# A two-block network on one core: in the second block the convolution's columns ahead of the keys, its norm beside the value and query projections, first scores ahead of the last query projection, one reciprocal for two heads

## The reference, cut to what matters

```python
h  = modulate(rmsnorm(x),   shift, scale)        # the block's tokens
hc = modulate(rmsnorm(ctx), shift_c, scale_c)    # 256 context tokens
z  = h @ w_in                                    # columns: q | k | v | gate u, gate v | conv a, conv gate
kc, vc = keys and values of hc                   # from the same columns k and v
att = softmax(q k^T / 8 + bias | q kc^T / 8) (v | vc)            # 8 heads of 64
sg  = gelu(u) * (w_s @ layernorm(gelu(v_s)) + b_s)               # spatial gating, 256 wide
cv  = silu(group_layernorm(dwconv31(a * sigmoid(gate)), 4 groups))   # 256 wide
x = x + mod * (concat(att, sg, cv) @ w_out)
x = rmsnorm(x + mod * conv_ffn(modulate(rmsnorm(x), ...)))
```

## Time and profile before

| | |
|---|---|
| median of three runs | 872.05 us |
| profiled execution | 870.56 us |
| its span on the core | 869.3 us |
| PE busy (share of the span) | 842.5 us (97%) |
| PE weight loads | 734.1 us (84%) |
| DVE busy | 600.8 us (69%) |
| ACT busy | 430.1 us (49%) |
| mean granted PE clock | 0.992 |
| second block's projections | 521 to 592 us of the span |
| attention | 592 to 634 us |
| output projection up to the feed-forward | 634 to 672 us |

### The profile page before, as it was taken

One profiled execution on the slowest core, in us unless ns is written; L12 is line 12 of the kernel. 1 busy time (PEld: TensorE's weight loads), 2 busy tenths in 40 slices (PEclk: granted clock), 3 DMA queues, 4 the chain that ended last, 5 costly groups with the idle time before them and its releaser, 6 DMA issues.

```text
span 869.3 us, 13540 instructions
## 1 busy us (share of the span) xinstructions
PE 842.5 (97%) x5555; PEld 734.1 (84%) x5555; DVE 600.8 (69%) x834; ACT 430.1 (49%) x662; POOL 52.7 (6%) x72
## 2 busy tenths in 40 slices
PE   9999999999999999999999999997898999999996
PEld 7988988869989999999988779984465999999995
DVE  7754547556698688688685765897766855665564
ACT  7555434446436646645636534634654644444432
POOL 8200004410000000000000000000000000000000
PEclk9999999999999999999999999999999999999999
DMA  8979865764543443345346776545446455555531
GB/s 286 322 228 269 237 213 213 274 220 150 157 131 107 135 146 118 126 146 178 113 146 211 261 260 241 197 146 178 161 170 218 134 175 180 191 194 188 176 121 49
DMA packets 102632, 160.10 MB, mean 184 GB/s; under 512 B 11317, under 2 KB 67993, under 8 KB 100266
## 3 DMA queue, kind: packets, MB, share of 16 engines
q1 hardware_dynamic: 102570, 159.24, 55.4%
HBM read 156.02 MB, written 3.21 MB: 183 GB/s over the span
## 4 chain that ended last, share of the span: by engine, by line
PE 81%; DVE 11%; ACT 3%; POOL 2%; issue 2%; DVEq 1%; POOLq 0%; ACTq 0%
PE acc L442 12%; PE acc L444 12%; PE acc L443 12%; PE acc L471 8%; PE acc L473 8%; PE acc L472 8%; PE misc L1167 4%; PE misc L2133 2%; PE misc L2135 2%; PE misc L2134 2%; DVE AT L1189 2%; DVE w_lo L415 2%; PE misc L854 2%; DVEq L1188 1%; PE misc L982 1%
## 5 line engine op out<-in xcount | busy, mean ns | idle before, releaser
L415 DVE TENSOR_TENSOR w_lo<-raw,w_hi 128x2048 fp32r<-128x2048 f32 x114 | 262.5, 2315 | 121.4 <-ACT w_hi L408 121.2
L408 ACT ACTIVATE w_hi<-raw 128x2048 fp32r<-128x2048 f32 x114 | 217.4, 1910 | 101.4 <-PE misc L2135 28.0
L442 PE MATMUL acc<-XH,w_hi 128*128 128x256 f32 x848 | 242.1, 286 | 1.1 <-DVE XL L597 1.1
L443 PE MATMUL acc<-XL,w_hi 128*128 128x256 f32 x848 | 240.3, 283 | 0.0
L444 PE MATMUL acc<-XH,w_lo 128*128 128x256 f32 x848 | 240.3, 283 | 0.0
L442 PEld LDWEIGHTS acc<-XH,w_hi 128*128 128x128 f32 x848 | 163.1, 192 | 3.8 <-issue 3.0
L443 PEld LDWEIGHTS acc<-XL,w_hi 128*128 128x128 f32 x848 | 163.1, 192 | 0.8
L444 PEld LDWEIGHTS acc<-XH,w_lo 128*128 128x128 f32 x848 | 163.0, 192 | 0.0
L471 PE MATMUL acc<-w_hi,XH 128*128 128x512 f32 (+1 forms) x224 | 87.4, 390 | 0.0
L473 PE MATMUL acc<-w_hi,XL 128*128 128x512 f32 (+1 forms) x224 | 85.7, 383 | 0.0
L472 PE MATMUL acc<-w_lo,XH 128*128 128x512 f32 (+1 forms) x224 | 85.5, 382 | 0.0
(11 more groups left out here) (284 smaller groups left out, 1282.9 us busy)
## 6 DMA issues: line engine op xcount, KB each, us to landing
raw<-in_hgrn_w_in_dram SPq DMA_DIRECT2D x32, 1024.0 KB, 5.5
ada_raw<-in_ada_w_dram SPq DMA_DIRECT2D x24, 1024.0 KB, 7.2
raw<-in_ffn_w_up_dram SPq DMA_DIRECT2D x22, 1024.0 KB, 5.0
raw<-in_pool_w_in_dram SPq DMA_DIRECT2D x15, 1024.0 KB, 6.0
raw<-in_ffn_w_down_dram SPq DMA_DIRECT2D x11, 1024.0 KB, 5.0
raw<-in_w_in_dram SPq DMA_DIRECT2D x10, 1024.0 KB, 5.4
raw<-in_pool_w_out_dram SPq DMA_DIRECT2D x8, 1024.0 KB, 5.1
raw<-in_hgrn_w_out_dram SPq DMA_DIRECT2D x8, 1024.0 KB, 5.1
```

The costliest lines, as they stand in the source:

```text
L408: self.hi_done.up(act.activation(self.w_hi[v % RING][:, 0:w], self.raw[j][:, 0:w], ACT.Copy), v)
L415: self.lo_done.up(dve.tensor_tensor(self.w_lo[j][:, 0:w], self.raw[j][:, 0:w], self.w_hi[v % RING][:, 0:w].bitcast(F32), ALU.subtract), v)
L442: pe.matmul(o, wh[:, k, c:c + P], xh[:, k, :], start=k == 0, stop=False)
L443: pe.matmul(o, wh[:, k, c:c + P], xl[:, k, :], start=False, stop=False)
```

## The change

It touches the second block only, and no product is added or left out.

- **Units.** The keys' slab has four tiles (the context's) instead of eight. The convolution follows; a new slab `kx` without units of its own reads the keys' two units again for the block's tokens, behind the convolution. So the order of loads is the same, and the keys' units stay in use longer.
- **`out1`.** The splits of the convolution's two units move ahead of each half's copy of turned tokens on ACT and behind each half's low part on DVE. PE turns the two halves after the second and the third context key.
- **`in2`.** PE: context keys, convolution, keys, gates, values; the context's value tiles are cut so that the group sum of the taps comes after the first unit of both, and the sum of the squares between the second units. The norm of the convolution, its silu and split run on DVE and ACT beside the value and query projections; the sum of squares is written over `CP`. The gating's layernorm takes two instructions per half instead of three. The first scores come ahead of the last query tile.
- **`attention`.** No group sums. One reciprocal takes the sums of both heads of a step. The low halves of convolution and gating follow step 0. Of the output projection's units DVE splits one ahead of the loop, and the other three after steps 1, 4 and 6; ACT splits its last two after steps 2 and 4. Modulation product 15 moves from step 1 to step 2.
- **`out2`.** Gating and convolution are taken first in every tile, the last heads last.

```diff
-        self.u_k = slab(8, *by_column(w_in2, 512))
+        self.u_k = slab(4, *by_column(w_in2, 512))
         self.u_cv = slab(4, *by_column(w_in2, 2048))
+        self.u_kx = slab(4)
+        self.slab[self.u_kx] = self.slab[self.u_k]
...
         for half in range(2):
+            self.hi(self.first(u0 + half, 3) + RING)
             for c in range(2):
                 self.act_high("in2", half, c, self.XH)
             self.act_context_key(2 + half)
-        self.hi(self.first(u0, 3) + RING)
-        self.hi(self.first(u0 + 1, 3) + RING)
...
             for c in range(2):
                 self.dve_low("in2", half, c, self.XH, self.XL)
-        self.lo(self.first(u0, 3) + RING)
-        self.lo(self.first(u0 + 1, 3) + RING)
+            self.lo(self.first(u0 + half, 3) + RING)
...
         for n in range(4):
             self.project(k, n, n * P, HC, KD)
-            if n == 3:
+            self.pe_ada(KD + n)
+            if n in (1, 2):
                 for c in range(2):
-                    self.pe_turn("in2", 0, c, self.XN2)
-            self.pe_ada(KD + n)
-        for c in range(2):
-            self.pe_turn("in2", 1, c, self.XN2)
+                    self.pe_turn("in2", n - 1, c, self.XN2)
         for n in range(4):
-            self.project(k, 4 + n, n * P, X, KD, self.both_ready("in2") if n == 0 else None)
+            self.project(cv, n, n * P, X, KD, self.both_ready("in2") if n == 0 else None)
         for n in range(4):
-            self.project(cv, n, n * P, X, KD)
+            self.project(kx, n, n * P, X, KD)
...
-        self.project_tokens(v, (2, 3), self.slab[v], 0, 512, HC)
+        self.project_tokens(v, (2, 3), self.slab[v][:1], 0, 512, HC, K=KD)
+        self.pe_group_mean()
+        self.project_tokens(v, (2,), self.slab[v][1:], 0, 512, HC, K=KD)
+        self.pe_group_square()
+        self.project_tokens(v, (3,), self.slab[v][1:], 0, 512, HC, K=KD)
...
         for n in range(4):
             self.project(q, n, n * P, X, KD)
+            if n == 2:
...
+                pe.wait_ge(self.V.h, self.V["gated2"])
+                self.pe_scores(0)
...
+        self.conv_taps(0, 8)
+        self.lo(self.first(k, 0) + RING)
+        self.conv_taps(8, 12)
+        self.lo(self.first(k, 1) + RING)
...
+        self.conv_taps(12, 16)
+        self.lo(self.first(cv, 0) + RING)
+        self.conv_taps(16, 18)
+        self.lo(self.first(cv, 1) + RING)
...
+        self.conv_taps(18, TAPS)
...
+        dve.wait_ge(self.A.h, self.A["cv_root"])
+        t = V.up(dve.reciprocal(self.CS, self.CS))
...
-    ADA_BESIDE = ((12, 13), (14, 15), (), (16,), (17,), (18,), (19,), ())
+    ADA_BESIDE = ((12, 13), (14,), (15,), (16,), (17,), (18,), (19,), ())
...
     def dve_normalize(self, s):
-        dve, V = self.nc.vector, self.V
+        dve, V, n = self.nc.vector, self.V, s % 2 * 2
+        dve.wait_ge(self.A.h, self.A["e", s, 1])
+        t = V.up(dve.reciprocal(self.soft[:, n:n + 2, 2:3], self.soft[:, n:n + 2, 1:2]))
+        dve.wait_ge(V.h, t)
         for e in range(2):
-            n = s % 2 * 2 + e
-            dve.wait_ge(self.A.h, self.A["e", s, e])
-            t = V.up(dve.reciprocal(self.soft[:, n, 2:3], self.soft[:, n, 1:2]))
-            dve.wait_ge(V.h, t)
...
+            if s == 0:
+                self.dve_mix("mix_conv", 6, self.CA)
+                self.dve_mix("mix_gate", 4, self.U)
...
+            if s in (1, 4, 6):
+                self.lo(v + (1, 4, 6).index(s) + 1)
...
-        self.pe_out2_part(0, 0, (4, 5))
+        self.pe_out2_part(0, 0, (4, 5, 6, 7))
...
-        self.pe_out2_part(1, 0, (4, 5, 0, 1, 2))
-        self.pe_out2_part(0, 0, (3, 6, 7))
+        self.pe_out2_part(0, 1, (4, 5, 6, 7, 0, 1, 2))
+        self.pe_out2_part(0, 0, (3,))
+        self.pe_out2_part(0, 1, (3,))
```

167 lines of the change are left out of this document (75 added, 92 removed).

## The result

| | before | after |
|---|---|---|
| median of the runs | 871.83 us (4 runs, 871.46 to 872.45) | 865.25 us (4 runs, 865.10 to 865.37) |
| profiled execution | 870.56 us | 865.37 us |
| its span | 869.3 us | 864.1 us |
| mean granted PE clock | 0.992 | 0.993 |

The changed kernel takes 0.9924 of the time of the kernel before (95% interval 0.9907 to 0.9941): **faster**, by a small amount that is clear of no change: 6.6 us between the medians and 5.2 us between the two profiled executions. The forecast was 867.1 us, with a gain of 4.9.

The account below looks back on a forecast made before the run. PE was taken to bound most of the kernel, a DVE-PE-ACT chain attention. Gains of 4.0 us (steps 1 to 5) and 0.85 (step 6) make 4.9, set against the 872.05 median: 867.1 us, range 864.8 to 870.4.

Parts of the forecast that it names:

- Step 1: Second block's projections: earlier turns and convolution columns first remove PE's waits of 1.07 and 0.2 us; gain 1.27 us.
- Step 2: Keys' units held 10 us longer delay later loads; first value unit lands after 8.3 us; cost 0.5, between 0 and 1.0.
- Step 3: Two group sums move from attention into the value projections, where PE is full: 1.12 and 1.02 us, cost 2.1 us.
- Step 4: First scores ahead of the last query projection: step 1's bias starts at 595.97 against 595.74, just enough to pay for the sums.
- Step 5: Attention: DVE is the bound with 33.2 us of work; PE reaches the output projection at 630.25, gain 4.0 including steps 1 to 4.
- Step 6: Output projection, convolution and gate first: the 0.7 us wait and some 0.15 of restart go, gain 0.85; nothing altered afterwards.
- The clock: Ahead of the feed-forward: the sum counted nothing for the clock's second fall, where PE idles 2.45 us.
- One sign of being wrong: In attention: the prediction would be wrong if DVE waits for scores or sums for more than 1 us.
- the clock did not fall in attention: Rival: the clock falls again in attention, 3.4 us at half speed, costing up to 1.7 us: 868.8 us, chance 0.20.
- One margin was thin: Rival: margins of 1.2 to 1.6 us at split handoffs are too thin; two late ones add 3 us: 870.1, chance 0.14.
- loads are not served together: Rival at the value units: queues share among loads, so the first value unit lands about 558: 873.4 us, slower, chance 0.05.
- fourth rival: More comes: value unit lands in 7.8 us or less and no clock fall ahead of the feed-forward: 865.3 us, chance 0.11.

Follow-up runs that it names:

- turns_back: Changed kernel with the two turns of the normalized input and their high and low halves in the old order: 869.85 us (1 run), 125.05 up to the output projection.
- ada_load_first: Changed kernel with one modulation weight load issued ahead of the two value units instead of behind them: 870.30 us (1 run), 127.35 up to the output projection.
- old_out2_order: Changed kernel with the output projection's products in the order of the kernel before: 863.49 us (1 run), 30.19 from the projection's start to the last residual.
- early_work: Changed kernel with two weight splits and the convolution's and gate's mixes moved into DVE's idle times ahead of the first two softmaxes: 861.16 us, 0.9884 of before.
- two_recips: Changed kernel with a reciprocal of its own for each head again, instead of one for two heads: 866.86 us, 0.9949 of before.
- splits_outside: Changed kernel with the output projection's weight splits back outside the attention steps, two ahead of the loop and two behind: 862.29 us, 0.9892 of before.
- moved_old_order: Changed kernel with DVE's work moved into idle times, the fourth split behind the loop and the output projection's old order: 861.34 us, 0.9878 of before.

## Why the prediction was right, step by step

The sign was right, the time lies inside the range, and the mechanism is the one foretold; but five of the six terms were mis-sized, and that the time of the profile came so close is luck in part, since a gain and a loss that the forecast missed nearly cancel.

- **Step 1** (turns and convolution first, 1.27): 1.54 measured by `turns_back`. The forecast took the sum of two waits, 1.07 and 0.2. The 0.27 beyond them is probably the restart behind a wait, which step 1 left out and step 6 counted; no row prices it alone.
- **Step 2** (the keys held longer, 0.5): a cost that did not come at all. The first value unit landed in 7.1 us, not 8.3, and there was no wait; with 8.3 PE would have waited some 0.8 us. The estimate took over the landing of the same unit before the change. The loads ahead of it were the same and stood at the same distances (the gates' unit 5.76 us ahead, two modulation loads between), and still it landed 1.2 us sooner. That is no scatter: 8.1 and 8.3 us in the two profiles with the kernel before's order, 7.0 to 7.2 in all eleven with the change's order of loads. What follows it differs, the second value unit 0.5 us behind it instead of 5.8; whether that is the reason no run shows. `ada_load_first` shows only what one megabyte more ahead costs, 2.5 us.
- **Step 3** (two sums, 2.1): 1.7. The timeline's durations overlap; the distance between starts is 0.86, the row's duration 1.02 to 1.12.
- **Step 4** (scores): 1.07, as its starts imply.
- **Step 5** (attention from scores(1) to the output projection, 594.7 to 630.25 = 35.55): 35.17. The stretch held to 1%, DVE's normalizations as well, at 0.99 us per step. Its two products fill 0.80 us between starts (596.95 to 597.75), so 0.40 each. The earlier trace rows had not shown two products in a row: there 0.40 stands between a product and the reciprocal behind it (598.05 to 598.45), so the step carried that distance over, rightly. By the rule of the Trainium skill ("VectorE: DVE Perf Modes", The DRAIN you can't avoid), that the next operation does not start until the pipe is empty, the stage would have been 1.1 us longer; the trace does not show it. The same section of the Trainium skill says that a next operation that is not held, that is, not made to wait for all earlier ones, starts earlier, which the forecast left out; the 0.40 agrees with that.
- **Steps 1 to 5** came to 5.43 instead of 4.02. The four errors above, 0.27 + 0.5 + 0.4 + 0.4, make 1.57 where 1.41 is to be explained; the other 0.16 us I can't place.
- **Step 6** (output projection, 0.85): PE gained 0.96 up to the modulation product that follows it (31.05 before, 30.09 after), but the last residual only 0.65. The new order gives 0.3 back on ACT and DVE, by a weight load that is issued 1.4 us later. "Nothing is altered from there on" was wrong in that point. And the wait for `MIXL` went with the early norm, not with the order, as `old_out2_order` shows.
- **The clock** ahead of the feed-forward was taken as unchanged; the fall was twice as long in the profiled execution and took 1.1 us.

The profiled executions therefore differ by 0.22 + 5.43 + 0.65 - 1.10 = 5.2 us, close to the forecast's 4.9 in part by a gain that it missed and a loss that it missed. The medians differ by 6.6: the profiled execution of before was 1.3 us under its median, that of after at its own. The forecast noticed this gap and set its 4.9 against the median; by medians it missed a quarter of the gain. Where the other 1.4 us (6.6 less 5.2) lie no row shows, since only the profiled executions have rows.

One sign of being wrong did appear by its letter: DVE waited over 1 us for scores, 4.11 and 2.56 us. Both waits lie ahead of the stretch that step 5 adds up, and step 4's own starts imply them, so they do not speak against the sum; from there on DVE's longest idle piece is 0.89 us.

Of the rivals, the clock did not fall in attention here (1.00 over the whole stretch), but did so once in another kernel of the study, at its price. One margin was thin, 0.4 us at the first value unit, and it held. The loads are not served together. The time came out at the fourth rival's 865.3, whose first half (the unit lands in under 7.8 us) happened and whose second half (no fall ahead of the feed-forward) did not: that agreement is luck.

What stays open is why that second fall is 3.4 us long in some profiles and 6.8 in others. TensorE's idle time in front of it does not sort them: 2.45 us with the short one before and in `old_out2_order`, but 2.68 and 2.72 with the short one in `turns_back` and `early_work`, and 2.68 and 2.71 with the long one in `two_recips` and `splits_outside`.

## What to carry to other kernels

Before you move work into a stage, ask which engine will bound that stage afterwards, and look for that engine's idle time just ahead of it: the change turned attention from a chain of waits into a stage with DVE busy for 92% of it, with three splits on top that had 6.7 us of idle DVE in front of them. Compare two kernels by the distance between marks inside one profile, which repeats to 0.14 us in the output projection here, while single runs of one kernel lie up to 6 us apart; and look at the granted clock in every stretch before a difference is put down to an edit. Where a transfer's landing decides, count the bytes issued ahead of it (one megabyte, 2.5 us), and give a landing that is taken over from another place in the program a spread of 1 us: the same loads ahead gave 8.3 and 7.1 us.

## What was unexpected

A wait on TensorE can be followed by a cost of nearly its own length: in one execution 1.96 us for a split, then a fall to 1.2 GHz that took 1.7 us more, though TensorE had been full up to the wait. The same fall comes in fixed sizes in these profiles, 3.4 or 6.8 us at half speed, and its price depends on how full TensorE is then: for the short one 1.7 us in the value columns and, in `moved_old_order`, in attention, where TensorE was full, and 1.1 ahead of the feed-forward, where TensorE waits for others in part of it. And an order that is better for the engine that waited can be worse for the end: the output projection's new order left PE's timing as it was and cost DVE 0.3 us, through a weight load that it lets start later.
